# Sparse attention: stationary values, scores two units ahead

## The reference, cut to what matters

```python
logits = einsum('bthd,btkd->bhtk', q, k_g) * d ** -0.5
logits = where(valid, logits, -1e30)
p = softmax(logits)                       # over the kept keys
o = einsum('bhtk,btkd->bthd', p, v_g)
```

## Time and profile before

| | us |
|---|---|
| median of 3 runs | 2935.43 |
| lowest, highest | 2932.95, 2937.0 |
| profiled execution | 2936.72 |
| its span | 2934.9 |
| TensorE, VectorE, ScalarE, POOL busy | 2782.6, 1781.5, 1238.0, 1188.1 |
| value matmuls (576), turns (288), busy | 72.5, 43.8 |

### The profile page before, as it was taken

The page is one execution under the profiler, slowest core; times in us unless marked ns, Lnnn a source line. Parts: engine busy times, 40 slices in busy tenths (PEclk is TensorE's granted clock), DMA queues, the critical chain, the costliest instruction groups (busy, mean ns, idle before and its releaser), DMA issues. The chain is left out here.

```text
span 2934.9 us, 38679 instructions
## 1 busy us (share of the span) xinstructions
PE 2782.6 (95%) x13600; PEld 2297.2 (78%) x13600; DVE 1781.5 (61%) x2680; ACT 1238.0 (42%) x2261; POOL 1188.1 (40%) x840
## 2 busy tenths in 40 slices
PE   5999999999999999999998889979999999999998
PEld 4877788787788888888787667868877888887877
DVE  6758757322676666622746888764457777776143
ACT  5225545101533333323544667545443444443243
POOL 4011222423634444534642143530073456665454
PEclk7999999999999999999999899989999999999999
DMA  6431111322422222254520123100051221224452
GB/s 247 159 115 30 29 44 51 103 77 96 141 72 72 86 86 86 74 182 157 181 96 8 37 69 105 44 8 1 29 191 52 81 86 65 77 86 165 151 183 90
DMA packets 176236, 272.33 MB, mean 93 GB/s; under 512 B 13145, under 2 KB 105561, under 8 KB 176089
## 3 DMA queue, kind: packets, MB, share of 16 engines
q1 hardware_dynamic: 176088, 270.39, 27.9%
HBM read 224.21 MB, written 46.14 MB: 92 GB/s over the span
## 5 line engine op out<-in xcount | busy, mean ns | idle before, releaser
L2069 POOL TENSOR_TENSOR sb_out_lo<-sb_out_raw,sb_out_hi 128x512 fp32r<-128x512 f32 (+1 forms) x174 | 309.3, 1783 | 450.6 <-ACT sb_out_hi L2056 450.5
L133 PE MATMUL psum<-sb_out_hi,sb_a_hi 128*128 128x512 f32 x912 | 360.2, 395 | 11.6 <-DVE sb_a_lo L2061 10.7
L134 PE MATMUL psum<-sb_out_lo,sb_a_hi 128*128 128x512 f32 x912 | 357.2, 392 | 0.0
L135 PE MATMUL psum<-sb_out_hi,sb_a_lo 128*128 128x512 f32 x912 | 357.2, 392 | 0.0
L1544 POOL TENSOR_TENSOR sb_pair_lo<-sb_pair_sum,sb_pair_hi 128x512 fp32r<-128x512 f32 x180 | 236.8, 1326 | 269.9 <-ACT sb_pair_hi L1686 269.9
L133 PE MATMUL psum<-sb_h_hi,sb_w_hi 128*128 128x512 f32 x640 | 258.9, 405 | 8.3 <-DVE sb_h_lo L2210 4.6
L135 PE MATMUL psum<-sb_h_hi,sb_w_lo 128*128 128x512 f32 x640 | 252.0, 394 | 0.0
L134 PE MATMUL psum<-sb_h_lo,sb_w_hi 128*128 128x512 f32 x640 | 251.8, 393 | 0.0
L133 PE MATMUL psum<-sb_h_hi,sb_pair_hi 128*128 128x512 f32 x576 | 224.1, 389 | 0.0
L134 PE MATMUL psum<-sb_h_lo,sb_pair_hi 128*128 128x512 f32 x576 | 224.1, 389 | 0.0
L135 PE MATMUL psum<-sb_h_hi,sb_pair_lo 128*128 128x512 f32 x576 | 224.1, 389 | 0.0
(11 more groups left out here) (482 smaller groups left out, 6422.7 us busy)
## 6 DMA issues: line engine op xcount, KB each, us to landing
act_kept<-sb_gate_up SPq DMA_DIRECT2D x40, 512.0 KB, 2.9
sb_pairs_raw<-in_w_up SPq DMA_DIRECT2D x18, 1024.0 KB, 5.3
sb_late_w<-in_w_ada SPq DMA_DIRECT2D x32, 512.0 KB, 4.8
sb_w_raw<-in_w_in SPq DMA_DIRECT2D x54, 256.0 KB, 3.2
sb_out_raw<-in_w_ffn_down SPq DMA_DIRECT2D x44, 256.0 KB, 3.0
sb_out_raw<-in_w_down SPq DMA_DIRECT2D x44, 256.0 KB, 2.8
sb_act_ring<-act_kept SPq DMA_DIRECT2D x40, 256.0 KB, 3.9
sb_act_late<-act_kept SPq DMA_DIRECT2D x40, 256.0 KB, 4.0
```

What stands on the lines that cost most here:

```text
L133: nc.tensor.matmul(out, stationary.hi, moving.hi, start=start, stop=False)
L134: nc.tensor.matmul(out, stationary.hi, moving.lo, start=False, stop=False)
L135: return nc.tensor.matmul(out, stationary.lo, moving.hi, start=False, stop=stop)
L2069: self.nc.gpsimd.tensor_tensor(w.lo, raw, w.hi.bitcast(F32), ALU.subtract).then_inc(self.w_lo, 1)
```

## The change

The value product is turned round: the 64 value columns are stationary, and the 128 turned probabilities move. The two heads of a pair go to the two halves of the array's columns and of bank 6's partitions, so that the result is already turned, `[head columns, queries]`. The values of a pair are split over two steps, the first half of the blocks at an even unit and the rest at the next. The row sums are no longer divided out on rows: VectorE inverts them (`inverted`), POOL widens each to 64 columns (`widen`), TensorE turns the widened sums (`turn_sums`), and VectorE multiplies. For t < 3 it first parks the product in a free part of `pT` (`taken`) and multiplies later out of PSUM (`scaled`); from t = 3 on ScalarE copies the turned sums (`turned_sums`) and `taken` multiplies straight into `attT`. `pT` has four places. The order inside a step changes: TensorE does scores(u+2), turn(u), and then half a pair's values; VectorE does maximum(u+2) ahead of the low copy of u, and waits in it for exponent(u).

```diff
-    def values(self, pe, u):
-        t, head = u // RH, u % RH
-        pe.wait_ge(self.t_out_act, u + 1)
-        if t >= 4:
-            pe.wait_ge(self.t_out_dve, u - 4 * RH + 1)
-        if head == 0 and t:
-            pe.wait_ge(self.o_ready, t)
-        for b in range(t + 1):
-            last = self.nc.tensor.matmul(self.core.ps[:, 6, head * HD:(head + 1) * HD], self.pT[:, u % 2, b, :], self.av[:, b, :], start=b == 0, stop=b == t)
-        last.then_inc(self.pv_done, 1)
+    def values(self, pe, u, half):
+        t, nc = u // RH, self.nc
+        middle = (t + 2) // 2
+        if half == 0:
+            pe.wait_ge(self.t_out_act, u + 2)
+            if t >= 4:
+                pe.wait_ge(self.t_out_dve, u - 4 * RH + 2)
+            if u % RH == 0 and t:
+                pe.wait_ge(self.o_ready, t)
+        for b in range(0, middle) if half == 0 else range(middle, t + 1):
+            for a in range(2):
+                head = u % RH + a
+                last = nc.tensor.matmul(self.core.ps[a * HD:(a + 1) * HD, 6, head // 2 * P:(head // 2 + 1) * P], self.av[:, b, :],
+                                        self.pT[:, (u + a) % 4, b, :], start=b == 0, stop=b == t)
+                if b == t:
+                    last.then_inc(self.pv_done, 1)
...
     def head(self, pe, u):
-        self.turn(pe, u)
-        if u:
-            self.values(pe, u - 1)
         if u + 2 < self.many:
             self.scores(pe, u + 2)
-
-    def turn_rows(self, pe, t):
-        pe.wait_ge(self.o_ready, t + 1)
+        self.turn(pe, u)
+        if u >= 2:
+            self.values(pe, u - 2 - u % 2, u % 2)
+
+    def turn_sums(self, pe, t):
+        pe.wait_ge(self.wide_ready, t + 1)
...
+        for j in range(4):
+            last = self.nc.tensor.transpose(self.core.ps[:, self.sums_bank(t), j * P:(j + 1) * P], self.over[:, 2 * j:2 * j + 2, :], self.cst["ident"])
+        last.then_inc(self.sums_turned, 1)
+
+    def widen(self, pool, t):
+        pool.wait_ge(self.sums_ready, t + 1)
         if t:
...
+            pool.wait_ge(self.sums_turned, t)
+        copy(self.nc, self.over[:, :, :], self.den[:, t, :].unsqueeze(2).to_broadcast([P, RH, HD]), self.cst).then_inc(self.wide_ready, 1)
 
     def maximum(self, dve, chain, u):
         nc, t, j = self.nc, u // RH, u % 2
         dve.wait_ge(self.s_done, u + 1)
+        if u >= 2:
+            dve.wait_ge(self.exp_done, u - 1)
...
+    def inverted(self, dve, t):
         dve.wait_ge(self.exp_done, (t + 1) * RH)
-        chain(nc.vector.reciprocal(sums, sums))
+        self.nc.vector.reciprocal(self.den[:, t, :], self.den[:, t, :]).then_inc(self.sums_ready, 1)
+
+    def taken(self, dve, t):
+        src = self.core.ps[:, 6, :].rearrange("p (j q) -> p j q", q=P)
         dve.wait_ge(self.pv_done, (t + 1) * RH)
...
+        if t < 3:
+            self.nc.vector.tensor_copy(self.kept(t), src).then_inc(self.o_ready, 1)
+        else:
+            dve.wait_ge(self.sums_out, t - 2)
+            self.nc.vector.tensor_tensor(self.attT[:, :, t * P:(t + 1) * P], src, self.inverse[:, :, :], ALU.mult).then_inc(self.o_ready, 1)
+
+    def scaled(self, dve, t):
+        dve.wait_ge(self.sums_turned, t + 1)
+        dve.wait_ge(self.o_ready, t + 1)
+        src = self.core.ps[:, self.sums_bank(t), :].rearrange("p (j q) -> p j q", q=P)
+        self.nc.vector.tensor_tensor(self.attT[:, :, t * P:(t + 1) * P], self.kept(t), src, ALU.mult).then_inc(self.at_out, 1)
 
     def rows_of(self, dve, chain, u):
+        if u + 2 < self.many:
+            self.maximum(dve, chain, u + 2)
         if u >= 4 * RH:
             self.turned_low(dve, u)
-        if u and u % RH == 0:
-            self.scaled(dve, chain, u // RH - 1)
-        if u + 2 < self.many:
-            self.maximum(dve, chain, u + 2)
+        if u % RH == RH - 1:
+            self.inverted(dve, u // RH)
+        if u > RH and u % RH == 1:
+            self.taken(dve, u // RH - 1)
...
-ROWS_AFTER = {23: 0, 25: 1, 27: 2, 33: 3, 41: 4, 49: 5, 57: 6}
+SUMS_AFTER = {23: 0, 25: 1, 27: 2, 32: 3, 40: 4, 48: 5, 56: 6}
...
-                att.values(pe, TB * RH - 1)
-                att.turn_rows(pe, TB - 1)
+                for half in range(2):
+                    att.values(pe, TB * RH - 2, half)
+                att.turn_sums(pe, TB - 1)
```

More of the change, by code:

```diff
@@ L3117, in __init__ @@
         self.sc, self.pr = lay(at, "scores", [P, 2, SEQ]), lay(at + 8, "probs", [P, 2, SEQ])
-        self.pT, self.ob = lay(at + 16, "probs_T", [P, 2, TB, P]), lay(at + 24, "out_rows", [P, 4, RH, HD])
-        small = lay(small_at, "sparse_small", [P, 4 + 2 * RH])
-        self.mx, self.neg, self.den = small[:, 0:2], small[:, 2:4], small[:, 4:4 + 2 * RH].rearrange("p (a h) -> p a h", h=RH)
+        self.pT = lay(at + 16, "probs_T", [P, 4, TB, P])
+        self.over, self.inverse = lay(at + 36, "inverse_sums", [P, RH, HD]), lay(at + 38, "inverse_turned", [P, 4, P])
+        small = lay(small_at, "sparse_small", [P, 4 + TB * RH])
+        self.mx, self.neg, self.den = small[:, 0:2], small[:, 2:4], small[:, 4:4 + TB * RH].rearrange("p (t h) -> p t h", h=RH)
         self.marked, self.many = marked, TB * RH
-        (self.s_done, self.s_free, self.neg_ready, self.exp_done, self.t_done, self.t_out_act, self.t_out_dve, self.pv_done, self.o_ready, self.ot_done,
-         self.at_out) = (core.sem(n) for n in ("att_scores", "att_free", "neg_ready", "exp_done", "probs_turned", "t_out_act", "t_out_dve", "pv_done",
-                                               "o_ready", "ot_done", "at_out"))
+        (self.s_done, self.s_free, self.neg_ready, self.exp_done, self.t_done, self.t_out_act, self.t_out_dve, self.pv_done, self.o_ready,
+         self.sums_ready, self.wide_ready, self.sums_turned, self.sums_out, self.at_out) = (core.sem(n) for n in (
+            "att_scores", "att_free", "neg_ready", "exp_done", "probs_turned", "t_out_act", "t_out_dve", "pv_done", "o_ready",
+            "sums_ready", "wide_ready", "sums_turned", "sums_out", "at_out"))
     def score_bank(self, u):
@@ L3130, in turn_bank, with sums_bank, kept @@
         return 4 if u >= 4 * RH else 3 if u > 21 and u % 2 == 0 else 7
-    def out_bank(self, t):
+    def sums_bank(self, t):
         return t % 2 if t < 3 else 7
+    def kept(self, t):
+        return self.pT[:, t, 4:TB, :]
     def scores(self, pe, u):
@@ L3140, in scores @@
             pe.wait_ge(self.at_out, 3)
+        if u == 4 * RH + 1:
+            pe.wait_ge(self.t_out_act, 4 * RH - 1)
         for at in range(0, SPAN[t], HALF):
@@ L3202, in turned_low @@
         dve.wait_ge(self.t_done, u + 1)
-        self.nc.vector.tensor_copy(self.pT[:, u % 2, 4:t + 1, :], self.core.ps[:, 5, 0:(t - 3) * P].rearrange("p (b q) -> p b q", q=P)).then_inc(self.t_out_dve, 1)
-    def scaled(self, dve, chain, t):
-        nc, sums = self.nc, self.den[:, t % 2]
+        if u < 4 * RH + 3:
+            dve.wait_ge(self.at_out, 3)
+        self.nc.vector.tensor_copy(self.pT[:, u % 4, 4:t + 1, :], self.core.ps[:, 5, 0:(t - 3) * P].rearrange("p (b q) -> p b q", q=P)).then_inc(self.t_out_dve, 1)
@@ L3241, in probs_of, with turned_sums @@
             self.exponent(act, u + 2)
[L3243 to L3246, removed]
+    def turned_sums(self, act, t):
+        act.wait_ge(self.sums_turned, t + 1)
+        if t > 3:
+            act.wait_ge(self.o_ready, t)
+        self.nc.scalar.activation(self.inverse[:, :, :], self.core.ps[:, self.sums_bank(t), :].rearrange("p (j q) -> p j q", q=P),
+                                  ACT.Copy).then_inc(self.sums_out, 1)
 EARLY = {4: ((), (0, 1)), 5: ((2, 3), (4, 5)), 6: ((6, 7), (8, 9)), 7: ((10, 11), (12, 13))}
 LATE = 14
-ROWS_AFTER = {23: 0, 25: 1, 27: 2, 33: 3, 41: 4, 49: 5, 57: 6}
+SUMS_AFTER = {23: 0, 25: 1, 27: 2, 32: 3, 40: 4, 48: 5, 56: 6}
 def spread_phase(core, h, wv, cos, sin, cst, bias, retention_of, spill, q_rows, q_tiles, tops, sparse_of, first_w, next_w, next_raw, next_first):
@@ L3569, in _ @@
                     att.rows_of(dve, chain, u)
-                att.scaled(dve, chain, TB - 1)
+                    if SUMS_AFTER.get(u, 3) < 3:
+                        att.scaled(dve, SUMS_AFTER[u])
+                att.taken(dve, TB - 1)
             @block.gpsimd
@@ L3614, in _ @@
                 split_tile(nc, pool, passed, next_hi, 1, next_raw, next_first, next_done)
+                for t in range(TB):
+                    att.widen(pool, t)
                 pool.wait_ge(next_done, 1)
@@ L3715, in _ @@
                         parts_out(TB - 1)
-                    if u in ROWS_AFTER:
-                        att.rows_out(act, ROWS_AFTER[u])
-                att.rows_out(act, TB - 1)
+                    if SUMS_AFTER.get(u, 0) > 2:
+                        att.turned_sums(act, SUMS_AFTER[u])
+                att.turned_sums(act, TB - 1)
 def small_layouts():
```

22 lines of the change are left out of this document (8 added, 14 removed).

## The result

The changed kernel takes 2915.03 us (median of four runs, 2910.88 to 2920.74) against 2936.22 beside it (2932.95 to 2937.86): a ratio of 0.993 [0.9915, 0.9945], 21.2 us less. Timed again later, five runs gave 2912.44 against 2935.98, 0.992 [0.9906, 0.9933]. The profiled execution took 2914.57, its span is 2912.8.

The account below looks back on a forecast made before the run. TensorE was taken to bound the stretch, after t = 3 nearly alone. Values -26.8, edges +16.2, order -9 and tail -0.5 sum to -20.1 us: 2916.6 profiled, some 2915 as a median; range 2898 to 2931.

Parts of the forecast that it names:

- Values: Value matmuls on TensorE: 0.117 us per block and head instead of 0.21, over 288 of them 26.8 us less.
- the old 0.105 a pass goes with the full 128-column load: Old value matmuls: 0.105 us a pass comes from the full 128-column stationary load, not from streaming 64 columns.
- Edges: Going in and out of the half-width form around each value group: net 0.27 us a unit, 60 units, 16.2 us more.
- rival of a hidden switch: Value groups: loads of the next form slip under the last pair, the 16.2 falls away, -36 us, 2899; chance 0.19.
- Scores ahead of the turn: TensorE's order: scores two whole units ahead of their turn remove the turns' waits, 9 us less.
- TensorE bounds the stretch, and after t = 3 nearly alone: Sparse attention, 1979 to 2112 us: from t = 4 on TensorE is busy 94 to 99% of each stage.
- What is late next: VectorE's low copy out of the single turn bank, behind a maximum; TensorE stays the bound with half a microsecond to spare.
- The rival that all of it comes back there: Wait for VectorE's low copy: its loop sets the units, some 12 of the 20 us are lost, 2927; chance 0.13.
- met long before: VectorE's maximum(u + 2) waiting for exponent(u): no delay expected, as scores and exponent are two periods apart.
- Sums, rows, tail, start: Widened sums' turns: no wait; scaling: 2 us more on VectorE; tail: about 0.5 us shorter; before 1979: 0, between -2 and +3.
- The clock: TensorE's granted clock: the forecast is wrong if it falls below 1.00 after 1997 us.

Follow-up runs that it names:

- order alone: The kernel before with the new order on TensorE and VectorE and the old values: 2925.02 us against 2936.7, ratio 0.9961.
- pairs ahead: Changed kernel with both halves of a pair's values in one group ahead of the odd unit's turn: 2905.95 us, ratio 0.9896; timed again 2907.17.
- values alone: The changed kernel with the old order on TensorE and VectorE: 2932.26 us, ratio 0.9984 to the kernel before.
- pairs behind: Changed kernel with both halves of a pair's values in one group behind the odd unit's turn: 2910.41 us, ratio 0.9915 to the kernel before.
- turn between: Changed kernel with half a pair's values ahead of the odd unit's turn and half behind it: 2907.45 us, ratio 0.9899 to the kernel before.
- copy first: Changed kernel with VectorE's low copy and sums ahead of the maximum again, TensorE's order new: 2912.06 us, ratio 0.9918 to the kernel before.

## Why the prediction came out, step by step

The median is the predicted one by luck, through errors that cancel: the sum of the steps was 20.1 us, the phase saved 27.8, and the profiled execution gave 4.5 of it back behind the phase and began it 1.2 later. For the phase the steps were 7.7 us short. From turn to turn 4.7 of that lie at t = 4 to 7, 1.8 in units 16 to 31 (7.1 saved, 5.3 forecast), 1.0 in the first 16 units and 0.2 in the tail. Most of the 1.8 may be the clock's, which was 0.91 and is 1.00 in half of these units.

| turn to turn | before | forecast | after |
|---|---|---|---|
| t = 4 | 21.1 | 17.3 | 17.1 |
| t = 5 | 23.9 | 20.0 | 19.4 |
| t = 6 | 26.8 | 23.7 | 22.0 |
| t = 7 | 25.5 | 22.0 | 19.8 |

*Values: right.* 0.112 us a pair against 0.117, so 288 x (0.21 - 0.112) = 28.2 where I had 26.8. The halves run side by side, and taking that away costs 18.7 us. That the old 0.105 a pass goes with the full 128-column load finds no support: with 64 columns loaded (and 128 moving) a pass in single file still takes 0.109.

*Edges: right in the unit.* Against the same unit with the old values and the new order (fence of the order alone) the turn is 0.10 longer up to the first value; the value group of six pairs takes 0.81, 0.14 over 6 x 0.112; the scores 0.01 more: 0.25 where I had 0.27, 14.5 us for the 58 groups and not 16.2. (How much is pair and how much edge is a choice: at 0.109 a pair the edge is 0.27 again, and the sum is the same.) The Trainium skill, "TensorEngine Tiling (Array Packing)", under Key Properties, says that a change of the tiling mode drains the engine. The trace agrees that the change costs time, 0.10 in and 0.14 out. So values and edges make -13.7 by the unit, and -14.4 by the phase behind the order alone; I had -10.6. Taking 26 edges away brought less than this price (pairs ahead). The rival of a hidden switch falls.

*Scores ahead of the turn: right in kind, too small.* I took 9 us; alone it brings 13.4. From turn to turn, as the step was worked out, t = 4 and t = 5 came as I had them (2.2 and 1.8); I left nothing at t = 6 and 7, where 1.1 and 2.2 were, and in the first 16 units, where 0.8 were. That is the largest of the mis-sized terms, 4.4 us.

*"TensorE bounds the stretch, and after t = 3 nearly alone": wrong.* It failed as the reading of the 94 to 99% of the earlier trace rows. A share of drawn busy time hides gaps under the matmuls' tails; the unit at t = 5 took 2.99 with 2.70 of work. I took this for slack to be cleared, of a size of its own, added to the values' gain. The runs show a loop that set the units as long as the old order stood: shortening the values alone left t = 4 at 21.0, and brought 1.3 and 1.2 at t = 6 and 7 instead of 3.4 and 3.7 behind the order. The sum held because the change does both; for the values alone the working gives 10.6, and the run gave 6.2 in the phase and 4.4 in the time.

*What is late next: right.* 0.4 us of turns wait for the low copy from t = 4 on. The rival that all of it comes back there falls, but two rearrangements of the values bring it up (0.9 and 5.7 us), so the margin is small, as priced. One detail is wrong: the wait of the maximum for the exponent of two units before is not "met long before". At t = 5 the maximum starts as that exponent ends, at 2035.00; TensorE does not wait for it.

```profile
2035.02 0.96 DVE L3218 CUSTOM_DVE_ANT_0 sb_scores<-psum,sb_bias 128x768 f32<-128x768 f32 x1 [0.76 <-ACT sb_probs L3262]
```

*Sums, rows, tail, start: right within a microsecond.* No turn of the sums waits. POOL's widening takes 1.04, below the 1.337 that I took as its neighbour:

```profile
L142 POOL TENSOR_TENSOR sb_inverse_sums<-sb_sparse_small,sb_ones 128x512 f32<-128x512 f32 x8 | 8.3, 1040 | 93.5 <-DVE sb_sparse_small L3232 86.6 <-PE psum L3200 6.9
```

The tail is 0.7 shorter (0.5 forecast), the first 16 units 1.0, in the second profile 0.4 (0, between -2 and +3).

*The clock.* It is 1.00 in the phase after 1997, as the steps needed. That it could rise in units 16 to 23 or fall behind the phase stood in no step.

**Open.** Whether the changed kernel meets the low clock behind the phase more often than the other kernels: of the profiles, the changed kernel's first, values alone and pairs behind have it (817.9, 816.1 and 815.5 behind the phase); its second and the remaining ones don't (812.1 to 814.2), so neither the new values nor the new order decides it alone. The granted clock of the whole launch, known for every execution, averages 0.975 over nine of the changed kernel, 0.976 over 31 of the kernel before and 0.978 over four of turn between; it fits such a difference, but does not say where in the launch it lies. The same may be why the changed kernel's median and phase disagree by some microseconds beside copy first and turn between; that is not shown. And why pairs ahead gain 3 us in the phase for 26 edges, and not 6.5, is shown only in part by its waits for VectorE.

## What to carry to other kernels

Before adding up an order's gain and a shorter operation's gain, ask whether the engine's units come at the sum of its parts: where they don't (2.99 against 2.70 here), a loop sets the pace, and what you shorten in one order comes back as a wait until the order is changed too. Where two heads can fill two halves of the array, put their passes next to each other; in single file all of the gain went here. Count the groups that change the array's form, and when merging them, look at what the neighbouring unit then has to cover its waits.

## What was not expected of the hardware

*Two halves in sequence still overlap.* In the kernel with one head after the other, a group of 24 passes begins at 2049.37; in the records of the single passes the first head's start up to 2050.62, but the second head's first starts at 2050.30. The group takes 2.38 us to the next turn, where 24 x 0.109 is 2.62:

```profile
2049.37 2.45 PE L3179 MATMUL psum<-sb_probs_T,sb_av 128*64 128x128 f32 x24
2051.75 0.98 PE L3166 MATMUL psum<-sb_consts,sb_probs 128*128 128x128 f32 x7
```

So, as this trace has it, passes to the other half of the array start while three of the first half's are still to start.

*The same idle stretch, another clock.* Behind equal waits of 2.05 to 2.3 us, in equal code, TensorE was granted the full clock in one execution and half of it for a while in another, 4.8 us in all between two profiles of the very same kernel.
